# State-space scans: rows of running sums by transfers, masked products in banks, and a new order of heads

## The reference

```python
X = (xs * dt[..., None]).reshape(b, c, t, g, e, p)             # chunks of t = 128 positions
a_cs = jnp.cumsum((dt * a).reshape(b, c, t, g, e), axis=2)      # running sums within a chunk
seg = a_cs[:, :, :, None] - a_cs[:, :, None, :]
decay = jnp.exp(jnp.where(lower, seg, -jnp.inf))
cb = jnp.einsum('bclgn,bcsgn->bclsg', Cc, Bc)
y_diag = jnp.einsum('bclsge,bcsgep->bclgep', cb[..., None] * decay, X)
...
y_off = jnp.einsum('bclgn,bcgepn->bclgep', Cc, s_in) * jnp.exp(a_cs)[..., None]
```

## Time and profile before

| | |
|---|---|
| median of 3 runs | 1684.62 us (1684.27 to 1687.24) |
| profiled execution | 1684.64 us |
| its span, first to last instruction | 1682.9 us |
| TensorE, VectorE, ScalarE, GpSimd busy | 99%, 60%, 40%, 41% |
| granted TensorE clock | 1.00 of full speed throughout (2.4 GHz) |
| moved by transfers | 147.34 MB, mean 88 GB/s |

### The profile page before, as it was taken

The page is one execution under the profiler, slowest core; times in us unless marked ns, Lnnn a source line. Parts: engine busy times, 40 slices in busy tenths (PEclk is TensorE's granted clock), DMA queues, the critical chain, the costliest instruction groups (busy, mean ns, idle before and its releaser), DMA issues.

```text
span 1682.9 us, 20420 instructions
## 1 busy us (share of the span) xinstructions
PE 1659.0 (99%) x8004; PEld 1316.8 (78%) x8004; DVE 1001.9 (60%) x1387; ACT 679.8 (40%) x932; POOL 687.4 (41%) x339
## 2 busy tenths in 40 slices
PE   7999999999999999999999999999999999999999
PEld 5777787878778888888877777788777788888887
DVE  5589859778774545422236898596788654545100
ACT  5445553344443333332244555533543433333221
POOL 3432223233445555554443222232334455555443
PEclk9999999999999999999999999999999999999999
DMA  5532111212223232322224221112123223222233
GB/s 167 129 96 74 62 63 63 76 63 64 87 88 100 88 100 88 100 92 94 91 88 126 85 73 63 63 63 76 63 66 96 89 88 100 89 100 90 93 99 107
DMA packets 43231, 147.34 MB, mean 88 GB/s; under 512 B 5152, under 2 KB 5920, under 8 KB 43136
## 3 DMA queue, kind: packets, MB, share of 16 engines
q1 hardware_dynamic: 42752, 145.28, 26.9%
q0 software_dynamic: 384, 0.75, 0.4%
HBM read 143.17 MB, written 2.85 MB: 87 GB/s over the span
## 4 chain that ended last, share of the span: by engine, by line
PE 89%; DVE 6%; issue 2%; ACT 1%; POOL 1%; DMA 0%; SPq 0%; DVEq 0%
PE banks L1080 27%; PE banks L1082 26%; PE banks L1081 26%; PE banks L1172 2%; PE banks L1151 2%; PE banks L1160 2%; PE banks L1255 1%; DVE sb_w_lo L747 1%; PE banks L1268 1%; PE banks L1227 1%; PE banks L1131 1%; DVE sb_e L822 1%; PE banks L1241 1%; PE banks L1211 0%; DVE sb_squares L735 0%
## 5 line engine op out<-in xcount | busy, mean ns | idle before, releaser
L360 POOL TENSOR_TENSOR sb_w_lo<-sb_w_raw,sb_w_hi 128x1024 fp32r<-128x1024 f32 x202 | 490.4, 2428 | 633.1 <-ACT sb_w_hi L453 633.1
L1080 PE MATMUL banks<-sb_h_hi,sb_w_hi 128*128 128x512 f32 x1360 | 558.2, 410 | 16.1 <-POOL sb_w_lo L360 10.7
L453 ACT ACTIVATE sb_w_hi<-sb_w_raw 128x1024 fp32r<-128x1024 f32 x258 | 272.6, 1057 | 671.4 <-PE banks L1082 665.1
L1082 PE MATMUL banks<-sb_h_hi,sb_w_lo 128*128 128x512 f32 x1360 | 537.3, 395 | 0.0
L1081 PE MATMUL banks<-sb_h_lo,sb_w_hi 128*128 128x512 f32 x1360 | 537.1, 395 | 0.0
L1080 PEld LDWEIGHTS banks<-sb_h_hi,sb_w_hi 128*128 128x128 f32 x1360 | 256.5, 189 | 99.5 <-issue 36.9
L1081 PEld LDWEIGHTS banks<-sb_h_lo,sb_w_hi 128*128 128x128 f32 x1360 | 256.9, 189 | 61.8 <-issue 6.9
L1082 PEld LDWEIGHTS banks<-sb_h_hi,sb_w_lo 128*128 128x128 f32 x1360 | 256.5, 189 | 60.1
L1045 DVE TENSOR_TENSOR banks<-banks,sb_rstd 128x512 f32<-128x512 f32 x88 | 61.5, 699 | 144.0 <-PE banks L1082 135.7
L1080 PE MATMUL banks<-sb_ff_hi,sb_w_hi 128*128 128x512 f32 x352 | 138.9, 395 | 0.0
L1082 PE MATMUL banks<-sb_ff_hi,sb_w_lo 128*128 128x512 f32 x352 | 138.9, 395 | 0.0
(11 more groups left out here) (199 smaller groups left out, 2326.9 us busy)
## 6 DMA issues: line engine op xcount, KB each, us to landing
sb_w_raw<-w_in SPq DMA_DIRECT2D x88, 512.0 KB, 3.4
sb_w_raw<-w_up SPq DMA_DIRECT2D x88, 512.0 KB, 3.3
sb_w_raw<-w_out SPq DMA_DIRECT2D x32, 512.0 KB, 3.4
...
```

Source lines behind the costliest of these rows:

```text
L360: g.tensor_tensor(WLO[:, n % 2, :], W[:, n % 2, :], WHI[:, n % 2, :].bitcast(F32), ALU.subtract).then_inc(w_lo.handle, 1)
L453: sc.activation(WHI[:, n % 2, :], W[:, n % 2, :], ACT.Copy).then_inc(w_hi.handle, 1)
L1080: mm(out, whi, hhi, start=start, stop=False)
L1082: return mm(out, wlo, hhi, start=False, stop=stop)
```

## The change

Rows that TensorE spread now come from HBM. At slot 4 SyncE stores the 64 rows of running sums (`T`) and of their exponentials (`exp_rows`, made by ScalarE) to a scratch tensor `sum_rows`. For each head it loads the two rows, repeated over 128 partitions, straight into the head's buffer (`head_rows`, 512 KB), and for each pair the exponentials into `EA` (`pair_exps`, two transfers of 192 KB). `row_sums`, `SEL`, `CS` and the exponential of the banks go. `seg` works in place: eight instructions of 128 columns, each subtracting a column's scalar and clipping. The freed banks 2 and 3 take the masked products, which were in SBUF. The heads' buffers are four instead of three. Of the order: the second group starts at slot 13 instead of 14; `seg` and `weigh` have tables of their own, `weigh` and the pairs stand one slot nearer the start of their group, `seg` of the first three heads one slot ahead of `weigh`; the gates of tiles 5 to 7 are in slots 21, 22 and 24 instead of 22, 24 and 25. TensorE still adds the odd heads' two directions.

```diff
@@ -102,9 +102,11 @@
-GROUP_AT = (2, 14)
-ROWS_AT = {GROUP_AT[h // 8] + 3 + h % 8: h for h in range(SSD_HEADS)}
-PAIR_AT = {GROUP_AT[t // 4] + 5 + 2 * (t % 4): t for t in range(SSD_HEADS // 2)}
+GROUP_AT = (2, 13)
+SEG_AT = {GROUP_AT[h // 8] + h % 8 + (1 if h % 8 < 3 else 2): h for h in range(SSD_HEADS)}
+WEIGH_AT = {GROUP_AT[h // 8] + 2 + h % 8: h for h in range(SSD_HEADS)}
+PAIR_AT = {GROUP_AT[t // 4] + 4 + 2 * (t % 4): t for t in range(SSD_HEADS // 2)}
@@ -193,7 +194,7 @@
                 ("x_tok", 40, [P, QT, 512], F32), ("s_in", 48, [P, 2, 3, SEQ], F32), ("b_tok", 60, [P, QT, P], F32),
-                ("cs", 62, [P, SEQ], F32R), ("exp_cs", 64, [P, 2, 2, 384], F32), ("cb", 70, [P, 2, SEQ], F32),
+                ("exp_rows", 62, [P, SEQ], F32), ("exp_cs", 64, [P, 2, 2, 384], F32), ("e_third", 70, [P, 2, SEQ], F32),
                 ("e", 74, [P, 2, 2, SEQ], F32), ("mh_sc", 82, [P, 4, SEQ], F32R), ("ml_sc", 90, [P, 4, SEQ], F32R),
@@ -206,8 +207,8 @@
     QHI, QLO, KHI, KLO = (rm[n] for n in ("q_high", "q_low", "k_high", "k_low"))
-    XT, SIN, BT, CS, EA, CB, E = (rm[n] for n in ("x_tok", "s_in", "b_tok", "cs", "exp_cs", "cb", "e"))
-    HEAD_E = (E[:, 0, :, :], E[:, 1, :, :], SQ[:, :, :])
+    XT, SIN, BT, ER, EA, E = (rm[n] for n in ("x_tok", "s_in", "b_tok", "exp_rows", "exp_cs", "e"))
+    HEAD_E = (E[:, 0, :, :], E[:, 1, :, :], rm["e_third"][:, :, :], SQ[:, :, :])
     SCC, CX, SCA, SCP, Z = (rm[n] for n in ("sc_c", "sc_cx", "sc_acc", "sc_prod", "z"))
@@ -225,13 +226,19 @@
+    CB = BANK[:, 2:4, :]
     scratch = nc.dram_tensor("bias_rows", [HEADS, COPIES, REL], F32).ap()
+    sum_rows = nc.dram_tensor("sum_rows", [2, 2 * DIR, SEQ], F32).ap()
     con_landed, setup_landed = sem("con_landed"), sem("setup_landed")
     gains_landed, par_landed = sem("gains_landed"), sem("par_landed")
     x_landed = [sem(f"x_landed{i}") for i in range(4)]
     x_stored = sem("x_stored")
-    sel_done, eps_done = sem("sel_done"), sem("eps_done")
+    eps_done = sem("eps_done")
+    rows_stored = sem("rows_stored", 32)
+    rows_landed = [sem(f"rows_landed{i}", 64) for i in range(4)]
+    ea_landed = [sem("ea_landed0", 128), sem("ea_landed1", 128)]
     bias_mm, bias_row = sem("bias_mm"), sem("bias_row")
@@ -269,7 +276,7 @@
-        return HEAD_E[h % 8 % 3]
+        return HEAD_E[h % 4]
@@ -305,6 +312,35 @@
             sp.dma_start(W[:, g % 2, 0:n], src[row, :, 0:n]).then_inc(w_landed[g % 2].handle, 16)
+        def store_rows():
+            sp.wait_ge(*cs_row.at(1))
+            sp.dma_start(sum_rows[0, :, :], T[0:2 * DIR, 0, :]).then_inc(rows_stored.handle, 16)
+            sp.wait_ge(*cs_exp.at(1))
+            sp.dma_start(sum_rows[1, :, :], ER[0:2 * DIR, :]).then_inc(rows_stored.handle, 16)
+        def head_rows(h):
+            grp, n = h // 8, h % 8
+            if h == 0:
+                sp.wait_ge(*rows_stored.at(32))
+                sp.wait_ge(*at_pv.at(UNITS))
+            if n % 4 == 3:
+                sp.wait_ge(*st_mm.at(6 * grp + 6))
+            if h >= 4:
+                sp.wait_ge(*y_mm.at(2 * ((h - 4) // 2) + 2))
+            rows = bass.AP(sum_rows.tensor, h * SEQ, [[0, P], [DIR * SEQ, 2], [1, SEQ]])
+            sp.dma_start(head_e(h), rows).then_inc(rows_landed[h % 4].handle, 16)
+        def pair_exps(t):
+            if t >= 2:
+                sp.wait_ge(*y_read.at(t - 1))
+            for d in range(2):
+                rows = bass.AP(sum_rows.tensor, (2 * DIR + DIR * d + 2 * t) * SEQ + (P, 0)[d], [[SEQ, 2], [0, 64], [1, SEQ - P]])
+                sp.dma_start(EA[:, t % 2, d, :], rows).then_inc(ea_landed[t % 2].handle, 16)
@@ -325,6 +361,13 @@
                     load(pos, a["w_in"], layer * C_DT + first + i)
+                slot = pos - POS["sc", 0]
+                if slot == 4:
+                    store_rows()
+                if slot - 2 in SEG_AT:
+                    head_rows(SEG_AT[slot - 2])
+                if slot - 1 in PAIR_AT:
+                    pair_exps(PAIR_AT[slot - 1])
                 if layer == 0 and (kind, i) == ("qk", 0):
@@ -419,16 +462,16 @@
                             scale_states(6 * grp + 2 * (s - GROUP_AT[grp]) + j)
-                if s in ROWS_AT and ROWS_AT[s] % 2 == 0:
-                    add_directions(ROWS_AT[s])
+                if s in WEIGH_AT and WEIGH_AT[s] % 2 == 0:
+                    add_directions(WEIGH_AT[s])
                 if s in PAIR_AT:
                     add_backward(PAIR_AT[s])
                 if s in (16, 17):
                     gate(2 * (s - 16))
                     gate(2 * (s - 16) + 1)
-                if s in (20, 22, 24):
-                    gate(s // 2 - 6)
-                if s == 25:
+                if s in (20, 21, 22):
+                    gate(s - 16)
+                if s == 24:
                     gate(7)
@@ -597,14 +640,8 @@
             for s, (kind, i) in enumerate(SLOTS):
-                if s in ROWS_AT:
-                    h = ROWS_AT[s]
-                    half = slice(64 * (h % 2), 64 * (h % 2) + 64)
-                    act.wait_ge(*seg_read.at(h + 1))
-                    if h >= 4:
-                        act.wait_ge(*y_read.at(h // 2 - 1))
-                    sc.activation(EA[half, (h // 2) % 2, :, :].rearrange("p d l -> p (d l)"),
-                                  BANK[half, 2:4, :].rearrange("p b s -> p (b s)")[:, P:P + 768], ACT.Exp).then_inc(ea_done.handle, 1)
+                if s in SEG_AT:
+                    h = SEG_AT[s]
                     act.wait_ge(*seg_done.at(h + 1))
@@ -618,7 +655,7 @@
                     sc.activation(T[0:64, 0, :], BANK[0:64, 2, :], ACT.Copy).then_inc(cs_row.handle, 1)
-                    sc.activation(CS[0:64, :], BANK[0:64, 2, :], ACT.Copy).then_inc(cs_hi.handle, 1)
+                    sc.activation(ER[0:64, :], BANK[0:64, 2, :], ACT.Exp).then_inc(cs_exp.handle, 1)
                     act.wait_ge(*dec_mm.at(1))
@@ -810,19 +845,14 @@
         def seg(h):
-            grp, n = h // 8, h % 8
-            dve.wait_ge(*ab_mm.at(h + 1))
-            if n >= 3:
-                dve.wait_ge(*y_mm.at(8 * grp + 2 * ((n - 3) // 2) + 2))
-            elif grp:
-                dve.wait_ge(*y_mm.at(8))
-            if n % 3 == 2:
-                dve.wait_ge(*st_mm.at(6 * grp + 6))
-            columns = AS[:, :, h:h + DIR + 1:DIR].rearrange("p c d -> p d c").unsqueeze(3).to_broadcast([P, 2, QT, P])
-            v.tensor_tensor(head_e(h).rearrange("p d (c l) -> p d c l", l=P),
-                            BANK[:, 2:4, :].rearrange("p d (c l) -> p d c l", l=P), columns, ALU.subtract).then_inc(seg_read.handle, 1)
-            dve.wait_ge(*seg_read.at(h + 1))
-            v.tensor_scalar(head_e(h), head_e(h), 80.0, None, ALU.min).then_inc(seg_done.handle, 1)
+            dve.wait_ge(*rows_landed[h % 4].at(16 * (h // 4 + 1)))
+            for d in range(2):
+                for c in range(QT):
+                    at = slice(P * c, P * c + P)
+                    ins = v.tensor_scalar(head_e(h)[:, d, at], head_e(h)[:, d, at], AS[:, c, column(d, h):column(d, h) + 1], 80.0,
+                                          ALU.subtract, ALU.min)
+            ins.then_inc(seg_done.handle, 1)
@@ -832,7 +862,7 @@
             dve.wait_ge(*yo_mm.at(t + 1))
-            dve.wait_ge(*ea_done.at(2 * t + 2))
+            dve.wait_ge(*ea_landed[t % 2].at(32 * (t // 2 + 1)))
             spans = (slice(P, SEQ), slice(0, SEQ - P))
@@ -853,8 +883,7 @@
                 return
-            if grp:
-                dve.wait_ge(*t_read.at(4))
+            dve.wait_ge(*(t_read.at(4) if grp else rows_stored.at(32)))
             col = 64 + column(d, 8 * grp)
@@ -943,8 +972,6 @@
                     at_low(3)
-                    dve.wait_ge(*cs_hi.at(1))
-                    v.tensor_tensor(CS[64:128, :], BANK[0:64, 2, :], CS[0:64, :].bitcast(F32), ALU.subtract).then_inc(cs_lo.handle, 1)
                     dve.wait_ge(*dec_exp.at(1))
@@ -1195,10 +1220,9 @@
                 pe.wait_ge(*y_read.at(4))
-                pe.wait_ge(*ea_done.at(8))
-                pe.wait_ge(*seg_done.at(8))
+                pe.wait_ge(*g_done.at(8))
             else:
-                pe.wait_ge(*cs_lo.at(1))
+                pe.wait_ge(*cs_exp.at(1))
                 pe.wait_ge(*cs_row.at(1))
@@ -1225,21 +1249,6 @@
             mm(bank(4 + d), BT[:, c, :], SQ[:, j % 2, :], start=True, stop=True).then_inc(st_mm.handle, 1)
-        def row_sums(h):
-            if h:
-                pe.wait_ge(*ea_done.at(h))
-                pe.wait_ge(*seg_read.at(h))
-            else:
-                pe.wait_ge(*cs_lo.at(1))
-                pe.wait_ge(*cs_col.at(1))
-            if h % 8 == 0:
-                pe.wait_ge(*tok_copied.at(5 * (h // 8) + 1))
-            if h == 0:
-                pe.wait_ge(sel_done.handle, 1)
-            for d in range(2):
-                ins = mm(bank(2 + d), SEL[:, column(d, h):column(d, h) + 1].to_broadcast([P, P]), CS[:, :], start=True, stop=True)
-            ins.then_inc(ab_mm.handle, 1)
```

31 lines of the change are left out of this document (12 added, 19 removed).

## The result

The changed kernel takes **1688.88 us** (median of 11 runs, 1686.92 to 1691.99), the kernel before 1684.45 in the same comparison. The ratio is 1.0027, with a 95% interval of 1.0018 to 1.0037: 4.4 us slower, small but beyond the 0.2% that can be told from no change. The forecast was 1675.0 us and faster. The time lies within its range (1665 to 1694), but the direction was wrong.

What follows compares the result with a forecast made beforehand. The prediction took TensorE, busy 99% of the span, to bound the kernel: 1684.64 less 19.3 us removed plus 9.6 us given back gave 1674.9, or 1675.0 us. The range was 1665 to 1694.

Steps and rivals of the forecast that it cites:

- The bound and what was removed: TensorE, busy 99% of the span, sheds 14.9 us of row sums and 4.4 of waits: 19.3 us in all.
- VectorE's own work: `seg` as eight instructions of 128 columns takes 1.7 us a head against 1.91 before; in the worse case 2.2.
- the sum by rows: Cost of `seg` worked out from profile rows: 0.287 us per 128-column instruction, 1.7 us for eight with overlap.
- Two engines carry the exponentials: Each pair's 393 KB go through two of sixteen DMA engines: 8.2 us at the better rate, 12.1 at the worse.
- one sign named for it: Time to landing of the exponentials: 6 us and more means two engines, 3 means sixteen.
- what the late rows give back: New waits of TensorE, mostly from rows queued behind exponentials: 2 x (0.5 + 3.5 + 0.8) = 9.6 us.
- Head 4's lateness: Rows about 4 us late for VectorE, absorbed by weights made ahead; some 0.5 us a layer given back at the group's end.
- Head 12's wait: Rows about 4 us late before slot 22's tile, waiting on VectorE's low half: 3.5 us a layer given back.
- Its row in the sum: At the products within chunks, GpSimd's gates still collide with VectorE: 0.8 us kept per layer.
- Rival 3: Slower: the two engines with the exponentials overflow TensorE's 14.5 us per two slots; 1694 at the mean rate; chance 0.22.
- Rival 1: Transfers are hidden, spread over 16 engines or less late; only 1.6 us come back: 1667; chance 0.20.
- Rival 2: VectorE takes the path over, 0.5 us more in 20 heads: 1685, no change; chance 0.12, with otherwise within 0.2%.

Runs made afterwards that it cites:

- the pair of runs with 4 and 2: Changed kernel with the exponentials in four transfers of 96 KB a pair, outermost source dimension 4 or 2: 1675.0 us with 4, 1692.0 with 2.

## Why the prediction was wrong, point by point

- **The bound and what was removed: right.** TensorE has 64 matmuls fewer. The 14.9 us of row sums hold, by the doubled sums. The waits before slot 7 and at the row sums are gone.
- **VectorE's own work: right.** The eight instructions take 1.66 us, median 0.28 each, as the sum by rows had it (1.7, 0.287 each). The fixed term of the Trainium skill (VectorE: DVE Perf Modes, "The TRN2 errata") gave 1.8; the trace stands nearer to the rows. That holds for the heads at which GpSimd rests; see below for the others. `weigh` stayed at 1.22 us in all 32 heads, and L416's block went, as the earlier trace rows suggested; in the run with masks in SBUF the loss of the bank operand costs 3.7 us, more than the wait of 1.8 that it was credited with.
- **Two engines carry the exponentials: right,** by the DMA share of 0.13 and by the pair of runs with 4 and 2. A pair takes 8.0 us there, the forecast's 8.2. But one sign named for it was useless: with sixteen engines these transfers land after 6.4 us too, where 3 was expected.
- **The step that failed: what the late rows give back.** The sum had 1.0 us before the group's end for head 4, 7.0 for head 12, 1.6 at the products within chunks and nothing for the clock, 9.6 in all. Measured are 5.6, 7.9, 3.7 and 6.4, in all 23.6. The 14.0 us between them are the whole error of 13.9. (One subtraction in that term is off as well: 1.5 us to spare less two row sums of 0.465 leave 0.6 and not 0.7, which changes nothing.) Three reasons:
  - *Head 4's lateness isn't absorbed.* The sum put it at about 4 us with 3.5 of them covered by weights made ahead. VectorE stood idle for 4.89 us, and TensorE then for 2.69. The lateness was nearly right; that it would be absorbed was wrong. What the sum left out is SyncE: the queue's next issue takes 3.81 us instead of 0.33 behind such a pair, so everything after it is late too. And `seg` stands in VectorE's queue ahead of the very low half that was to be the cover.
  - *The clock.* Head 12's wait had nearly the right size (3.9 and 4.0 us for 3.5), one tile earlier than forecast and with z's bank as releaser in place of the weights. Behind it TensorE ran at 1.2 GHz for up to 6 us. The kernel before, whose waits were all under 1 us in this stretch, never showed that, and the forecast priced waits alone: it put the clock at nothing without a reason.
  - *GpSimd beside `seg`.* Its row in the sum was 1.6 us, "GpSimd's gates still collide with VectorE there". The collision was in the right place but was sized by the old code, where the larger half of `seg` read a bank. The changed `seg` reads and writes SBUF alone and is held up most of the time that GpSimd works beside it: 4.5 us instead of 1.66. Measured in this row are 3.7 us; 0.64 of them stand at pair 3 of the first layer and stay when GpSimd is held, so 3.0 are GpSimd's. The Trainium skill states a rule for this (SBUF — State Buffer, "SBUF: two separate sides": VectorE and GpSimd share one pair of ports, which is held for a whole instruction while the other engine fully waits; for VectorE it concerns certain fast operations and those with two inputs in SBUF); the traces of both orders agree, with 4.51 and 6.60 us for the last head.
- **The rivals.** Rival 3 had the sign (slower) and the queue right. Its mechanism, an overflow at every pair, didn't happen: TensorE waits at heads 4 and 12 only, not at twelve places. Rival 1 (hidden, 1667) is what the kernel becomes once both causes are taken away: 1668.05. Rival 2 shows no part of its own: with sixteen engines and GpSimd held, TensorE's waits on VectorE in the two scans are 3.0 us in all.
